# Further token blocks of four experts gathered and transposed together, with block-major token tables

## The reference, cut to what matters

```python
N_EXPERTS, TOP_K, N_EXPERT_GROUPS, TOPK_GROUPS = 64, 8, 8, 4
EXPERT_FF, MOE_BLOCK = 256, 128
def body(acc, blk):
    rows, rw, e = blk
    xb = x_pad[rows]
    h = jax.nn.silu(xb @ w_gate[e]) * (xb @ w_up[e])
    yb = (h @ w_down[e]) * rw[:, None].astype(xb.dtype)
    return acc.at[rows].add(yb), None
...
shared = (jax.nn.silu(xf @ ws_gate) * (xf @ ws_up)) @ ws_down
return (acc[:T] + shared).reshape(B_, S, D)
```

## Time and profile before

| | before |
|---|---|
| median of 3 runs | 1633.97 us (1632.95 to 1635.86) |
| the profiled execution's own time | 1633.34 us |
| its span in the profile | 1631.7 us |
| PE busy | 1567.5 us (96%) |
| DVE busy | 1178.9 us (72%) |
| ACT busy | 1033.5 us (63%) |
| POOL busy | 506.6 us (31%) |
| DMA data moved | 368.63 MB |

### The profile page before, as it was taken

One profiled execution on the slowest core, in us unless ns is written; L12 is line 12 of the kernel. 1 busy time (PEld: TensorE's weight loads), 2 busy tenths in 40 slices (PEclk: granted clock), 3 DMA queues, 4 the chain that ended last, 5 costly groups with the idle time before them and its releaser, 6 DMA issues.

```text
span 1631.7 us, 32189 instructions
## 1 busy us (share of the span) xinstructions
PE 1567.5 (96%) x8246; PEld 1309.8 (80%) x8247; DVE 1178.9 (72%) x2037; ACT 1033.5 (63%) x1706; POOL 506.6 (31%) x495
## 2 busy tenths in 40 slices
PE   6999999999999999989999999999999999999986
PEld 6897888888887788778888888888888888888763
DVE  4215777777777788836877787777876787888866
ACT  3215666666666654526777787767776777878754
POOL 0000000000000125532554454543454454454426
PEclk9999999999999999999999999999999999999995
DMA  7223322222123434557999999999999999999987
GB/s 246 91 81 91 72 53 65 58 64 71 45 71 104 161 144 146 221 192 267 330 312 323 304 354 366 342 289 274 333 328 286 286 358 327 352 367 362 368 250 281
DMA packets 161321, 368.63 MB, mean 226 GB/s; under 512 B 53010, under 2 KB 73490, under 8 KB 161266
## 3 DMA queue, kind: packets, MB, share of 16 engines
q1 hardware_dynamic: 136272, 284.21, 49.7%
q0 software_dynamic: 24992, 83.73, 19.7%
HBM read 294.39 MB, written 65.11 MB: 220 GB/s over the span
## 4 chain that ended last, share of the span: by engine, by line
PE 73%; DVE 8%; DMA 7%; issue 5%; ACT 3%; ACTq 2%; POOL 1%; SPq 0%; DVEq 0%; POOLq 0%
PE bank_pair L1031 6%; PE bank_pair L1025 6%; PE bank_pair L1028 6%; DMA sums_scratch<-ys,sidx 6%; PE q_ps L91 4%; PE q_ps L93 4%; PE q_ps L92 4%; PE out_ps L916 4%; PE k_ps L894 3%; PE out_ps L1084 3%; PE out_ps L1085 3%; PE q_ps L1015 3%; PE k_ps L1052 2%; PE k_ps L1053 2%; PE k_ps L1060 2%
## 5 line engine op out<-in xcount | busy, mean ns | idle before, releaser
L1918 DVE TENSOR_TENSOR gu_lo<-raw_gu,gu_hi 128x1024 fp32r<-128x1024 f32 x260 | 306.4, 1220 | 28.0 <-ACT gu_hi L1396 27.8
L1396 ACT CAST gu_hi<-raw_gu 128x1024 fp32r<-128x1024 f32 x260 | 253.6, 1049 | 7.1 <-DMA raw_gu<-in_moe_w_up_dram 7.1
L1025 PE MATMUL bank_pair<-gu_hi,xb_hi 128*128 128x512 f32 x576 | 233.9, 406 | 5.3 <-DVE gu_lo L1918 3.9
L1028 PE MATMUL bank_pair<-gu_lo,xb_hi 128*128 128x512 f32 x576 | 227.7, 395 | 0.0
L682 POOL DMA_INDIRECT sums_scratch<-ys,sidx x63 | 120.8, 1917 | 152.9 <-DMA sums_scratch<-ys,sidx 118.9
L1918 DVE TENSOR_TENSOR dn_lo<-raw_dn,dn_hi 128x1024 fp32r<-128x1024 f32 x130 | 152.6, 1213 | 2.8 <-ACT dn_hi L1396 2.3
L1031 PE MATMUL bank_pair<-gu_hi,xb_lo 128*128 128x512 f32 x576 | 144.0, 392 | 3.8 <-DVE xb_lo L1922 3.8
L1025 PEld LDWEIGHTS bank_pair<-gu_hi,xb_hi 128*128 128x128 f32 x576 | 110.6, 192 | 28.6 <-issue 5.8
L613 POOL IOTA e<- 128x64 f32 x1 | 0.2, 185 | 427.5 <-DVE xs L1714 427.5
L1396 ACT CAST dn_hi<-raw_dn 128x1024 fp32r<-128x1024 f32 x130 | 130.0, 1052 | 4.2 <-DMA raw_dn<-in_moe_w_down_dram 4.2
L1301 ACT CAST pt_hi<-k_ps 128x512 fp32r<-128x512 f32 (+1 forms) x192 | 85.8, 482 | 73.5 <-PE k_ps L894 72.8
(11 more groups left out here) (307 smaller groups left out, 3967.5 us busy)
## 6 DMA issues: line engine op xcount, KB each, us to landing
raw_gu<-in_moe_w_gate_dram SPq DMA_DIRECT2D x128, 512.0 KB, 7.0
raw_gu<-in_moe_w_up_dram SPq DMA_DIRECT2D x128, 512.0 KB, 9.1
raw_dn<-in_moe_w_down_dram SPq DMA_DIRECT2D x128, 512.0 KB, 8.7
wqk<-in_fox_w_in_dram SPq DMA_DIRECT2D x66, 128.0 KB, 2.5
v_scratch<-v_out SPq DMA_DIRECT2D x32, 256.0 KB, 2.8
va<-v_scratch SPq DMA_DIRECT2D x16, 512.0 KB, 4.6
fin<-sums_scratch SPq DMA_DIRECT2D x16, 512.0 KB, 9.5
xs<-in_x_dram SPq DMA_DIRECT2D x8, 512.0 KB, 7.3
```

Source lines behind the costliest of these rows:

```text
L1025: i = pe.matmul(o3, xb_hi[s][:, c], g_hi[:, :, c], start=c == 0, stop=False, skip_group_check=True)
L1028: pe.matmul(o3, xb_hi[s][:, c], g_lo[:, :, c], start=False, stop=False, skip_group_check=True)
L1396: a.copy(hi, raw).then_inc(S[done], 1)
L1918: dve.tensor_tensor(lo, raw, hi, ALU.subtract).then_inc(S[lo_ok], 1)
```

## The change

**Tables.** The columns of `tab` are now block-major: first all experts' first blocks, then all experts' first further blocks, and so on (column block * 64 + e). Only the first 128 columns are loaded to the chip.

**One gather for four experts.** The first further blocks of experts 4n to 4n+3 are 4 x 32 = 128 places. VectorE lays their index columns out as `fidx` (one column per group), during the last shared block. `gather_four(n)` copies one column and gathers 128 rows at once into `x_rows_of_four`. With `bounds_check` the unused places, whose token number is past the last token, are skipped; VectorE has cleared the buffer once. Group 0 is gathered after the shared expert, ahead of expert 2's rows; group n + 1 is gathered within expert 4n + 1.

**One transposition for four experts.** `turn_four` is eight full 128x128 transposes into `k_ps`, in the middle of `gate_up` of the group's first expert. ScalarE casts the whole 128x1024 to the high columns of `xo` between its third and fourth gate and up pieces, and VectorE subtracts for the low columns behind its third piece and copies the weights. `xo` is now as wide as four experts' further blocks, and the matmuls L1084 and L1085 (now L1117 and L1118) take 128-column slices of it. The two per-block transposes, casts and subtractions go.

**What else.** A second and later further block of an expert, which this input doesn't have, is gathered, turned and split on its own (`gather_again`, `turn_again`), with its index column read from memory; a second running sum in `count_blocks` counts these. Some semaphores are merged. The loops now hold four experts: 836 rows of the order on PE where there were 411, 358 instead of 163 on VectorE, 311 instead of 141 on ScalarE, 261 instead of 152 on GpSimd.

```diff
-            tab = sb("tab", [P, TAB], I32, c=m)
+            tab = sb("tab", [P, 2 * E], I32, c=m)
+            xo = sb("xo", [P, DC * 2 * P + 2 * XR], F32R, c=m)
+            xo_of = xo[:, 0:DC * 2 * P].rearrange("p (c j s r) -> p c j s r", j=FOUR, s=2, r=XR)
+            fidx = sb("fidx", [P, E // FOUR], I32, c=m)
...
+            def gather_four(n):
+
+                if static(n) and n == 0:
+                    pool.wait_ge(S["extra_ok"], 4 + FOUR)
+                else:
+                    pool.wait_ge(S["fx_lo_ok"], 2 * n)
                 stand(pool)
-                g.tensor_copy(gidx[2][0:XR], tab[0:XR, ds(e * TAB_BLOCKS + k + 1, 1)]).then_inc(idx_ok[2], 1)
-                pool.wait_ge(idx_ok[2], x + 1)
+                g.tensor_copy(fidx_g[:], fidx[:, ds(n, 1)]).then_inc(idx_ok[2], 1)
+                pool.wait_ge(idx_ok[2], n + 1)
                 stand(pool)
-                g.indirect_dma_start(out=xg[2][par * XR:(par + 1) * XR], out_offset=None, in_=rows_dram,
+                g.indirect_dma_start(out=xgx[:], out_offset=None, in_=rows_dram,
+                                     in_offset=bass.IndirectOffsetOnAxis(ap=fidx_g[:, 0:1], axis=0), bounds_check=T - 1, oob_is_err=False
+                                     ).then_inc(S["fx_in"], 16)
...
+                if j == 1 and not (static(four) and four == E // FOUR - 1):
+                    gather_four(four + 1)
...
+            def turn_four(n, m):
+
+                pe.wait_ge(S["fx_in"], 16 * n + 16)
+                pe.wait_ge(S["scaled"], m - 1)
                 stand(pe)
-                rows = slice(par * XR, (par + 1) * XR)
-                v = strided(xg[2][rows, 0:D])
+                turn_rows(xgx, k_ps).then_inc(S["fx_turned"], 1)
...
                 for c in range(DC):
-                    pe.matmul(o3, xo[:, c], g_hi[:, :, c], start=c == 0, stop=False, skip_group_check=True)
-                    i = pe.matmul(o3, xo[:, c], g_lo[:, :, c], start=False, stop=c == DC - 1, skip_group_check=True)
-                i.then_inc(S["x_gated"], 1)
+                    rows = xo[:, (FOUR * c + j) * 2 * XR:(FOUR * c + j) * 2 * XR + P]
+                    pe.matmul(o3, rows, g_hi[:, :, c], start=c == 0, stop=False, skip_group_check=True)
+                    i = pe.matmul(o3, rows, g_lo[:, :, c], start=False, stop=c == DC - 1, skip_group_check=True)
+                i.then_inc(S["x_product"], 1)
...
+                if j == 0:
+                    pe.wait_ge(S["fx_lo_ok"], 2 * four + 1)
+                    stand(pe)
...
-                    turn_further(par, xi + nx - 1)
                     down(m - 1, par, e + 1)
...
+            def rows_of_four_hi(n):
+                act.wait_ge(S["fx_turned"], n + 1)
+                a.copy(xo[:, 0:DC * 2 * P].rearrange("p (q s r) -> p q s r", s=2, r=XR)[:, :, 0], k_ps[:].rearrange("p (q r) -> p q r", r=XR)
+                       ).then_inc(S["fx_hi_ok"], 1)
...
+            def rows_of_four_lo(n):
+                dve.wait_ge(S["fx_hi_ok"], n + 1)
+                q = xo[:, 0:DC * 2 * P].rearrange("p (q s r) -> p q s r", s=2, r=XR)
+                dve.tensor_tensor(q[:, :, 1], k_ps[:].rearrange("p (q r) -> p q r", r=XR), q[:, :, 0], ALU.subtract).then_inc(S["fx_lo_ok"], 1)
+                dve.tensor_copy(w_four[:], xgx[:, ds(FOUR * n + D, FOUR)]).then_inc(S["fx_lo_ok"], 1)
```

More of the change, by code:

```diff
@@ L74 @@
 XR = P // 4
+FOUR = P // XR
 BIAS_TILES = TT // 2
@@ L762, in expert @@
                 return xi, nx
-            expert(0, 0, "first")
-            expert(1, 1, "")
-            with pool.Fori(1, E // 2 - 2) as i:
-                for par in range(2):
-                    expert(2 * i + par, par, "")
-            expert(E - 4, 0, "")
-            expert(E - 3, 1, "", ahead=False)
-            expert(E - 2, 0, "last", ahead=False)
-            xi, nx = expert(E - 1, 1, "last", ahead=False)
+            for j in range(FOUR):
+                expert(j, j, 0, "" if j else "first")
+            with pool.Fori(1, E // FOUR - 1) as i:
+                for j in range(FOUR):
+                    expert(FOUR * i + j, j, i, "")
+            for j in range(FOUR):
+                expert(E - FOUR + j, j, E // FOUR - 1, "" if j < 2 else "last", ahead=j < 1)
             for what, t in LAST_POOL:
@@ L1163, in _, with expert @@
                     logits(TT - 1)
-            def expert(e, par, last=False):
+            def expert(e, j, four, last=False):
+                par = j % 2
                 w = 1 - par
@@ L1176, in turn_next, with rows_of_four @@
                         turn_rows(xg[1 - par], q_ps).then_inc(S["turned"], 1)
+                def rows_of_four():
+                    turn_four(four, m)
+                between = None if j else rows_of_four
                 with pe.If(before_it > 0):
@@ L1217, in expert @@
                 return xi, nx
-            with pe.Fori(0, E // 2 - 1) as i:
-                for par in range(2):
-                    expert(2 * i + par, par)
-            expert(E - 2, 0)
-            expert(E - 1, 1, last=True)
+            with pe.Fori(0, E // FOUR - 1) as i:
+                for j in range(FOUR):
+                    expert(FOUR * i + j, j, i)
+            for j in range(FOUR):
+                expert(E - FOUR + j, j, E // FOUR - 1, last=j == FOUR - 1)
         @block.scalar
@@ L1585, in expert, with four_experts @@
                     a.copy(bank_pair[:], b2[:]).then_inc(S["y_hi_ok"], 1)
-            counts = load_counts(0)
-            expert(0, 0, "first", counts)
-            expert(1, 1, "", counts)
-            with act.Fori(1, E // 2 - 1) as i:
-                counts = load_counts(2 * i)
-                for par in range(2):
-                    expert(2 * i + par, par, "", counts)
-            counts = load_counts(E - 2)
-            expert(E - 2, 0, "", counts)
-            expert(E - 1, 1, "last", counts)
+            def four_experts(e0, four):
+                for j in range(FOUR):
+                    if j % 2 == 0:
+                        counts = load_counts(e0 + j)
+                    pos = "first" if static(e0) and e0 + j == 0 else "last" if static(e0) and e0 + j == E - 1 else ""
+                    expert(e0 + j, j, four, pos, counts)
+            four_experts(0, 0)
+            with act.Fori(1, E // FOUR - 1) as i:
+                four_experts(FOUR * i, i)
+            four_experts(E - FOUR, E // FOUR - 1)
             for t in range(TT):
```

270 lines of the change are left out of this document (159 added, 111 removed).

## The result

| | before | after |
|---|---|---|
| median | 1633.46 us (4 runs, 1630.55 to 1635.86) | 1736.14 us (4 runs, 1735.28 to 1741.17) |
| ratio | | 1.0636 (95%: 1.0609 to 1.0663) |
| span of the profiled execution | 1631.7 us | 1733.9 us |
| PE busy | 1567.5 us (96%) | 1581.0 us (91%) |
| packets on the instruction queue q14 | 29 | 235 |

A forecast was written before the change was run, and what follows sets the result against it. PE was taken to bound the kernel, with 73% of the chain, until scatters set the pace from 1490 us. Savings of 35.7 and 6 us less the added costs gave -11.0 us: 1623 us, range 1613 to 1637.

The forecast's parts named there:

- the sum of -11.0 us: All terms added: -35.7 - 6 + 12.6 + 4 + 5.5 + 5.2 + 2.4 + 1 us.
- the first rival: Loops of four experts no longer stay loaded, each of 15 passes fetches again: 1624 to 1653 us, chance 0.18.
- Eight small transposes: On PE, eight 32-row transposes less per further block, 1.19 us each for thirty blocks: -35.7 us.
- The waits for xo: Six PE waits before L1084 for the further rows' low part, of which five go whole: -6 us.
- Eight full transposes in the middle: Eight 128-row transposes inside gate and up of a group's first expert, 0.9 us each for fourteen groups: +12.6 us.
- case (a): Ten group starts where the expert before has a further block: PE waits 0.4 us each, +4 us.
- Case (b): Group starts 12, 44, 48 without a further block before: PE waits about 2.4 us, +5.5 us (3 to 9).
- the second rival: Waits eat the saving, through the lower clock or the last experts' shifts: 1630 to 1633 us, chance 0.12.
- The first group: At expert 0, PE waits 5.2 us for the first gather of four, then the lower clock costs 2.4 us.
- The table: The smaller table load and the clearing of the group's rows hide behind the last shared block: no cost.
- the last part: Where the scatters of the sums set the pace, late group starts shift them: +1 us (0 to 4).
- Transfers: Rival: weights on the nearly always busy queues set the pace, so less PE work gives nothing: 1633 us, chance 0.06.

The follow-up runs named there:

- n_all: The changed kernel with the loops of ScalarE, VectorE and GpSimd written as pairs, PE's left at four experts: 1635.65 us, ratio 1.0004 to the kernel before.
- best: The changed kernel, three engines' loops as pairs, first gather of four issued sooner, the four's cast and subtraction after the first weight piece: 1618.20 us, 0.9902.
- the padded kernels: The kernel before with 170, 270 or 400 never-executed instructions at the end of ScalarE's loop: 1634.40, 1957.44 and 1960.37 us.

## Why the prediction was wrong, point by point

**The step that failed:** the sum of -11.0 us has no term for the loops' code, which was taken to stay loaded, and the first rival, which didn't take it so, priced one stop far too low. With that its chance and the end of the range were wrong. The mechanism was named: larger loop bodies, loaded again on each pass, packets on the instruction queues. But one stop was bounded at 1 to 2 us, from ScalarE's stand of 2 us in the earlier trace rows, which is a stand with the code loaded: it bounds nothing. A stand with loading was 7 to 8 us, and PE lost (1736.14 - 1635.65) / 14 = 7.2 us per turn of the loop with it. At that price the rival is 1623 + 100 = 1723 us, and the terms below make up the rest to 1736; 1624 to 1653 excluded both. The trace of before had no row for the price, and the right thing was to leave the range wide above or to say that nothing bounds it. The chance of 0.18 was too low too: bodies had about doubled on three engines and grown from 152 to 261 on GpSimd, and the arguments against were that the smaller ones stayed loaded and that by the rule cited there 311 and 358 might still fit.

**What held.** With the loops short the rest of the sum can be read off, in `n_all`, where the distance from expert 0's to expert 63's L1061 is 806.9 us and was 815.7:

- *Eight small transposes*: 14.17 - 12.98 = 1.19 us per further block, as taken.
- *The waits for xo*: four distances of 15.34 and one of 14.97 became 12.97, 11.5 us less in all, of which 6.0 are the transposes: 5.5 us in five.
- *Eight full transposes in the middle*: the distance 9.34 of the earlier trace rows became 10.27 in the changed kernel: 0.93 us, against 0.9. These are the rows of expert 55 and 56 (the view ends at 1593 us, so it counts six of the eight matmuls of the second):

```profile
1581.59 1.98 PE L1057 MATMUL bank_pair<-gu_hi,xb_lo 128*128 128x512 f32 x8
...
1591.86 1.53 PE L1057 MATMUL bank_pair<-gu_hi,xb_lo 128*128 128x512 f32 x6
```

- *Group starts of case (a)*: 0.24 to 0.57 us each and 0.40 in the mean of ten, as forecast (where the distance also holds the 1.2 us of the small transposes, they are taken out).

**Terms that were too small**, all seen without the loading:

- *Case (b)*: 4.5 and 4.3 us at experts 12 and 48 instead of 1.7, and at 44 3.2 us more than forecast. The wait was 3.33 instead of 2.4. VectorE ended its three pieces about 0.5 us later against PE than forecast, ScalarE having stood 2.55 us at its loop's start where it had stood 2.06 in the kernel before, and 0.8 us lie between the end of `w_four`'s copy (932.49 + 0.16) and PE's matmul, for which the sum had nothing. Then PE ran at the lower clock, which took about 1.6 us more at expert 12. That clock was in the second rival at 2.8 us a place. Some of it should have been in the sum, since the wait forecast there was nearly three times the 0.9 us that the rival's counter-argument leaned on.
- *The first group*: expert 0's matmuls, from the first L1049 to L1057, took 13.61 us and 3.73 before (L1025 to L1031): 9.9 us instead of 8.5. The gather took 6.0 us to land, although most of its places are skipped; the 4 us taken for that were too few.

```profile
762.26 1.06 POOL L679 DMA_INDIRECT x_rows_of_four<-rows_scratch,fidx_g  x1 [0.91 <-POOL fidx_g L676]
...
768.24 1.94 PE L1039 MATMUL k_ps<-ident,x_rows_of_four 128*128 128x128 f32 x8 [6.73 <-DMA x_rows_of_four<-rows_scratch,fidx_g]
```

- *The table* was put at nothing; the traces say about 3 us. The scatters that fill it were not weighed at all, though each block of GpSimd's list waits for them.

Between the profiles of the kernel before and of `n_all` (spans 1631.7 and 1634.9 us) the balance closes. The three places of (b) before the last part are 8.7 us over the forecast and the first group 1.6 (19.49 us from the last shared block's L1061 to expert 0's, where it was 9.35). The time up to the last shared block is 5.4 us longer, of which 3 are the table's by the reading above. The last part, from expert 55 on, is 0.5 us shorter, where 1 longer was forecast. That is 8.7 + 1.6 + 5.4 - 1.5 = 14.2 us, from -11.0 to +3.2. The change without its longer loops is worth nothing, and with the orders of `best` about 16 us.

**The other rivals.** Transfers did not bind: `n_all` and `best` have the same bytes and differ by 17 us. The Trainium skill ("Runtime: NRT & Kernel Launch", section "Instruction fetch mechanics") speaks of a window of two pages of 256 instructions and of a stall for a branch out of it. The direction is right here, and PE's body of 836 under its 2048 loads nothing, as the Trainium skill has it. That a body of 311 is loaded again in both places tried is not what this window leads one to expect. By its figures, as an estimate, 311 instructions reach into a third block of 256 only if they begin in the last 54 places of one, and two beginnings 129 apart can't both lie there.

## What to carry to other kernels

Count the instructions of every loop body, per engine, before and after a change that unrolls further; where the body grows and no trace shows one of that size, take the price of loading as unknown and not as small. When several engines load again at the same turn, each hides the others: shorten all, or the test says that none matters (here 6 and 15 us for one, 100 for all three). Packets on the instruction queues inside the loop's time, divided by engine with such tests, tell which loops are loaded again, also those that cost nothing, as GpSimd's did here. A nested loop with a branch gives a period of four the code of a period of two.

## What the runs showed of the hardware that I had not expected

A turn of a loop whose code is loaded again cost 7.2 us here and 10.8 us in the padded kernels, with the data queues at 58.9 and 32.9% of the DMA engines' time in the changed kernel. Bodies of 141 and 168 instructions on ScalarE, 214 on VectorE and 138 on GpSimd stayed loaded; 261 on GpSimd and 311, 413 and 543 on ScalarE did not, but 313 with 170 of them jumped over did. A gather of 128 places that skips most of them landed after 6.0 and 7.9 us, no sooner than the full one of the earlier trace rows with 5.6. PE waits of 2.74, 3.33 and 3.91 us, and a stand of 1.86, were followed by the lower clock; one of 0.35 us at 878 us in `n_all` was not.
